# Linear attention before convolution in layer two of block 2: the order of three branches in a two-block fp32 kernel

## The chip, the cores and the metric

The kernel runs on one core of a Trainium2 chip. The metric is the device time of one execution in microseconds (us).

## The reference

Two blocks of two layers each work on 256 tokens of width 1024, batch 1, in fp32. Block 1 mixes three kinds of attention and is not touched. Block 2 takes block 1's output `x` and 256 context tokens. Each of its layers normalises both and projects them to a row of 15 chunks; three branches work on the chunks and are merged:

```
ya = conv_module(val, glu, gate)      # depthwise, 31 taps, layer norm, silu gate, @ w_conv_out
yb = gla_branch(...)                  # chunked linear attention, both directions, @ w_gla_out
yc = attn_branch(...)                 # 8 heads, keys of context and latent tokens, @ w_attn_out
merged = sigmoid(p13) * ya + sigmoid(p14) * yb + sigmoid(p15) * yc
xs = xs + gate_x * (merged @ w_out)   # layer one does the same for the context tokens
```

The sum has three terms and can be formed in any order. In layer two the context serves only as keys, values and state: the outputs are those of the 256 latent tokens.

## The kernel before

**Work and units.** Tokens lie in tiles of 128: tiles 0 and 1 are latent, 2 and 3 context. Layer one of block 2 works on four tiles throughout, layer two on four for the keys, values and decays and on two for the rest. Weights come in pieces of 256 rows by up to 512 columns (512 KB). A piece is loaded by SyncE's queue into one of four buffers (`w_raw`), split by ScalarE (`cut_hi`, L1749) and VectorE (`cut_lo`, L2131) into a high and a low part, for which there are three buffers, and multiplied on TensorE in three products, high by high, low by high, high by low (L1398 to L1400 in `project`, L1416 to L1418 in `project_t`). A chunk is four pieces. With two tiles, a `project` step is one tile and one piece, 6 matmuls of 512 columns; a `project_t` step is one block of 128 channels and one piece, 6 matmuls of 256 columns.

**The branches.** The convolution is numbered 0, linear attention 1 and attention 2. Branch 0 needs CGATE (its gate, by `project_t`), 1 needs GG, 2 needs AG. Each then has two chunks of merge gates, M0A and M0B, M1A and M1B, M2A and M2B, whose sigmoid goes to the `sigma` buffer (`ev_sig`, L1968), and an output product y0, y1 or y2 in two halves of two pieces each. `ev_y` multiplies a product with its sigma (L2485 for the branch that comes first, which writes `merged` directly, L2487 for the others) and `acc_add` on GpSimd (POOL) adds the others to `merged` (L2770).

**What runs beside them.** Linear attention is a chain across all engines: decays and their sums (L1576, L1584, L1593), transposes of queries and keys (L1313, `gla_kt` L2511), scores within a chunk (L1615), states (L1628, L2537), outputs (L1646, L1652), then a norm that ends in `gla_n` (L2559). The convolution is 124 taps on VectorE in layer two, 31 for each of four channel blocks (L2442, L2445), then a mean, a variance, a norm and the gate (`conv_g`, L2763), and a split into high and low (`conv_hi` L2005, `conv_lo` L2476). Attention has 8 maps for each of two query tiles: scores L1683, maximum, exponential (L2073), transpose (L1313), values (L1707).

**What sets the order.** `Plan` holds lists of steps. `second_main` is the main list: in layer two VAL, GLU, KKV, LRQ, GV and AQ, then the branches in the order of `BRANCHES`:

```
    for i in BRANCHES[l]:
        first, second = MERGE[i]
        if i == 0:
            yield from project_t(l, CGATE)
            yield from inp(first, tiles, sigma)
        elif i == 1:
            if l == LAYERS - 1:
                yield from inp(GG, tiles, gated)
            yield [("gated", l, GG, t) for t in tiles]
            yield from beside(inp(first, tiles, sigma), cut(i), 2)
        ...
        yield from y(i, 0)
        yield from inp(second, tiles, sigma)
        yield from y(i, 1)
```

`cut(i)` yields the transpose of each tile of the branch's gated result (`flip y1` or `flip y2`, L1313), and `beside(..., 2)` sets one behind every second step of the chunk. `gated` (POOL, L2776) multiplies the normalised result with the gate and comes ahead of the transpose. Linear attention, taps, convolution's end, head norms and attention are further lists. Each list is cut into lanes, one for each engine; a lane keeps its order. `Plan.order` plays the program through with estimated lengths (`LENGTH`) and always takes the step that can start first, ties by `rank`, in which taps come last and projections behind most others. The result is one fixed sequence for each engine, so on the chip a step that waits holds up all that stands behind it on its engine.

**Banks.** PSUM has eight banks: 0 to 3 for projections and output products (`proj2`), 4 to 6 for the rest, 7 for sums. The four blocks of CGATE hold all four projection banks from their first matmul until `ev_cg` (L1957) has read them. `ev_cg` writes to `b.cg`, which lies over the taps' source `conv_u`, and so waits for the last tap. `ev_gate` of GG (L1978) and `ev_sig` have no such wait. All branches of layer two share one buffer for their split operand, `b.y[1]`. `conv_hi` of layer two has no wait of its own for y1; it comes behind `conv_g`, which needs `ev_cg`.

**Pieces.** `Plan.weights` numbers the pieces in the order in which the lists use them and keeps for each the last step that reads it, which the load and the split of a later piece wait for. There are 304.

Of the kernel before, what the change touches and what calls it, by code (L numbers as in the profile page):

```python
# [84 lines left out]
MOD_COLS = 2 * 3 * KD  # L85
MERGE = [(M0A, M0B), (M1A, M1B), (M2A, M2B)]

BRANCHES = [(1, 0, 2), (0, 1, 2)]


def sigma_before(layer, c):

    order = [MERGE[i][half] for i in BRANCHES[layer] for half in range(2)]
    at = order.index(c)
# [3 lines left out]
def branch_before(layer, i):  # L98
    at = BRANCHES[layer].index(i)
    return None if at == 0 else BRANCHES[layer][at - 1]  # L100

# [195 lines left out]
def branch(kind):  # L297
    def steps(l, c, t):
        return [("ev_y", kind, l, c, t)] + ([] if int(kind[1]) == BRANCHES[l][0] else [("acc_add", kind, l, c, t)])
    return steps  # L300
# [19 lines left out]
def second_main(l):  # L320
# [13 lines left out]
    else:  # L334
# [5 lines left out]
        yield from inp(AQ, tiles, evacuate2)  # L340
    for i in BRANCHES[l]:
        first, second = MERGE[i]
# [147 lines left out]
class Plan:  # L490
# [10 lines left out]
    def weights(self):  # L501

        for _, steps in self.queues:
            for step in steps:
                if step[0] not in ("project", "project_t", "mod"):
                    continue
                name = step[1:5] if step[0] == "project" else ("in2", *step[1:4]) if step[0] == "project_t" else step[:4]
                if self.piece_of.get(name) is None or self.piece_of[name] != len(self.pieces) - 1:  # L510
                    self.piece_of[name] = len(self.pieces)
                    self.pieces.append(name)
                    self.last_step.append(step)
                self.last_step[-1] = step
        first_of_2 = next(n for n, name in enumerate(self.pieces) if name[0] == "in2")
        self.raw_slot, self.cut_slot, self.raw_before, self.cut_before = [], {}, [], {}
        self.raw_done, self.arrived = [], []
        in_raw, in_cut, loads, cuts, cutting = {}, {}, {}, 0, []
        for n, name in enumerate(self.pieces):
            if n == first_of_2:  # L520
                cuts = 0
            raws, slots = (RAW1, CUT1) if n < first_of_2 else (RAW2, CUT2)
            raw = (n if n < first_of_2 else n - first_of_2) % raws
            self.raw_slot.append(raw)
            self.raw_before.append(in_raw.get(raw))
            in_raw[raw] = n
            loads[raw] = loads.get(raw, 0) + 16
            self.arrived.append((f"weights_in{raw}", loads[raw]))
            if name[0] == "mod":
                self.raw_done.append(self.last_step[n])  # L530
                continue
            cut, cuts = cuts % slots, cuts + 1
            self.cut_slot[n], self.cut_before[n], in_cut[cut] = cut, in_cut.get(cut), n
            cutting += [("cut_hi", n), ("cut_lo", n)]
            self.raw_done.append(("cut_lo", n))
        self.queues += [(0, cutting), (0, [("load", n) for n in range(len(self.pieces))])]
# [1192 lines left out]
def scalar_engine(k):  # L1729
# [229 lines left out]
    def ev_sig(l, c, t):  # L1959
# [5 lines left out]
        else:  # L1965
            i, half = earlier
            act.wait_ge("ev_y" if i == BRANCHES[l][0] else "acc_add", f"y{i}", l, half, t)
        do(b.sigma[:, t, :], ps[:, :], ACT.Sigmoid).then_inc(sem["ev_sig"], 1)  # L1968
# [1084 lines left out]
```

## Time and profile before

| | us |
| --- | --- |
| median of 3 runs | 1483.71 |
| lowest and highest | 1481.89, 1485.86 |
| the profiled execution, its own time | 1480.43 |
| span of that execution | 1479.1 |
| TensorE busy | 1350.5 (91%) |
| VectorE busy | 865.4 (59%) |
| ScalarE busy | 632.1 (43%) |
| GpSimd busy | 283.4 (19%) |
| mean granted TensorE clock | 0.938 |

The rows further down are of the profiled execution; their times count from the start of its span. Engines are PE (TensorE matmul), PEld (its weight loads, which overlap PE), DVE (VectorE), ACT (ScalarE), POOL (GpSimd) and SP (SyncE, which issues the loads). A granted clock of 1.00 is 2.4 GHz, 0.50 is 1.2 GHz. A matmul's duration in the rows includes its way through the array, so neighbours overlap: the distance of two starts is what one costs in a dense row of them. "idle before <- releaser" is what ended the time in which an engine did nothing; "issue" is idle time for which the trace shows no wait.

### The profile page before, as it was taken

The page shows a single profiled execution, that of the slowest core. Times are in us where ns is not written, and L with a number is a line of the kernel's source. Part 1 is how long each engine was busy: PE and PEld are TensorE (multiplying, and loading weights), DVE is VectorE, ACT ScalarE, POOL GpSimd, SP SyncE. Part 2 cuts the span into 40 slices and gives each one's busy share as a digit, 9 for nine tenths or more (in the row PEclk, how much of TensorE's full clock was granted, in tenths as well). Part 3 has the DMA queues.
Part 4 walks back from the last instruction along what each step waited for, and adds up shares of the span by engine and source line. Part 5 has one row for each costly group of instructions (what it writes and reads, how often), then busy time and mean ns, then how long its engine had stood idle before and what let it go on. Part 6 is the DMA issues. An engine that isn't in the chain of part 4 may idle for free.

```text
span 1479.1 us, 18892 instructions
## 1 busy us (share of the span) xinstructions
PE 1350.5 (91%) x7490; PEld 1065.2 (72%) x7490; DVE 865.4 (59%) x1469; ACT 632.1 (43%) x1007; POOL 283.4 (19%) x224
## 2 busy tenths in 40 slices
PE   5999787999782999997999999999999979989997
PEld 4877675877671777776676887777898766667886
DVE  3885644885647233488996432234676796544554
ACT  3444623444625164322536442333562550556452
POOL 0200101200105221237000011311351251000112
PEclk9999897999895999999999999999999995799999
DMA  9542537432534221121111222223453220023552
GB/s 336 166 131 88 191 104 304 156 129 86 190 107 148 67 81 48 59 71 57 57 58 33 68 72 96 89 86 107 151 172 104 91 91 3 15 92 116 182 181 83
DMA packets 48040, 165.19 MB, mean 112 GB/s; under 512 B 5734, under 2 KB 6950, under 8 KB 47696
## 3 DMA queue, kind: packets, MB, share of 16 engines
q1 hardware_dynamic: 47952, 163.98, 33.9%
q8 instruction: 59, 0.97, 0.3%
q14 instruction: 29, 0.24, 0.1%
HBM read 162.91 MB, written 1.05 MB: 111 GB/s over the span
## 4 chain that ended last, share of the span: by engine, by line
PE 70%; issue 14%; DVE 7%; POOL 4%; DMA 3%; ACT 2%; SPq 0%; POOLq 0%; DVEq 0%; ACTq 0%
PE bank L1398 15%; PE bank L1399 14%; PE bank L1400 14%; PE bank L1313 3%; PE bank L1683 3%; PE bank L1707 2%; PE bank L1416 2%; PE bank L1417 2%; PE bank L1418 2%; DVE conv_val L2445 2%; DMA w_raw<-in_wm 2%; PE bank L1646 1%; PE bank L1652 1%; PE bank L1628 1%; DVE w_lo L2131 1%
## 5 line engine op out<-in xcount | busy, mean ns | idle before, releaser
L2131 DVE TENSOR_TENSOR w_lo<-w_raw,w_hi 128x1024 fp32r<-128x1024 f32 (+3 forms) x256 | 316.9, 1239 | 299.4 <-ACT w_hi L1749 299.0
L1398 PE MATMUL bank<-w_hi,x_hi 128*128 128x512 f32 (+4 forms) x1120 | 459.2, 410 | 14.5 <-DVE x_lo L2476 5.9
L1749 ACT ACTIVATE w_hi<-w_raw 128x1024 fp32r<-128x1024 f32 (+3 forms) x256 | 263.6, 1031 | 466.2 <-PE bank L1400 264.4
L1399 PE MATMUL bank<-w_lo,x_hi 128*128 128x512 f32 (+4 forms) x1120 | 430.7, 385 | 0.0
L1400 PE MATMUL bank<-w_hi,x_lo 128*128 128x512 f32 (+4 forms) x1120 | 430.6, 385 | 0.0
L1398 PEld LDWEIGHTS bank<-w_hi,x_hi 128*128 128x128 f32 x1120 | 214.7, 192 | 67.3 <-issue 16.3
L1400 PEld LDWEIGHTS bank<-w_hi,x_lo 128*128 128x128 f32 x1120 | 213.1, 190 | 42.9
L1399 PEld LDWEIGHTS bank<-w_lo,x_hi 128*128 128x128 f32 x1120 | 214.2, 191 | 36.1
L2445 DVE SCALAR_TENSOR_TENSOR conv_val<-conv_u,par,conv_val 128x512 f32<-128x512 f32 (+1 forms) x240 | 153.7, 691 | 0.0
L2770 POOL TENSOR_TENSOR merged<-merged,sigma 128x512 f32<-128x512 f32 x24 | 37.3, 1586 | 168.1 <-DVE sigma L2487 168.1
L1416 PE MATMUL bank<-x_hi,w_hi 128*128 128x512 f32 (+1 forms) x192 | 67.5, 352 | 0.4 <-ACT conv_val L1942 0.4
L1417 PE MATMUL bank<-x_hi,w_lo 128*128 128x512 f32 (+1 forms) x192 | 64.7, 337 | 0.0
L1418 PE MATMUL bank<-x_lo,w_hi 128*128 128x512 f32 (+1 forms) x192 | 64.7, 337 | 0.0
L2073 ACT ACTIVATE att_p<-bank,att_stat 128x512 f32<-128x512 f32 (+1 forms) x48 | 29.4, 615 | 60.4 <-DVE att_stat L2621 60.3
L1332 PE MATMUL bank<-w_raw,mod_c_padded 128*32 128x128 f32 x768 | 30.5, 303 | 26.8 <-DMA w_raw<-in_wm 26.7
L1707 PEld LDWEIGHTS bank<-gla_k_att_kv,att_pt 128*128 128x128 f32 x320 | 44.1, 202 | 9.5 <-issue 5.0
L1683 PE MATMUL bank<-att_k_t,att_q_t 64*128 64x512 f32 (+1 forms) x96 | 49.0, 616 | 0.5 <-DVE att_q_t L2611 0.5
L2763 POOL TENSOR_TENSOR conv_val<-conv_val,conv_u 128x512 f32<-128x512 f32 (+1 forms) x8 | 8.4, 1070 | 196.8 <-ACT conv_u L1957 155.7
L1332 PEld LDWEIGHTS bank<-w_raw,mod_c_padded 128*32 128x32 f32 x768 | 21.5, 119 | 33.1 <-issue 17.4
L1416 PEld LDWEIGHTS bank<-x_hi,w_hi 128*128 128x128 f32 x192 | 36.4, 190 | 9.4 <-issue 5.7
L1707 PE MATMUL bank<-gla_k_att_kv,att_pt 128*128 128x64 f32 x320 | 43.1, 280 | 0.0
L1394 PE MATMUL bank<-bias_parts,bias_sel 96*128 96x512 bf16 (+2 forms) x78 | 30.2, 387 | 12.8 <-DVE bias_parts L2387 12.8
(339 smaller groups left out, 1904.2 us busy)
## 6 DMA issues: line engine op xcount, KB each, us to landing
w_raw<-in_w SPq DMA_DIRECT2D x168, 512.0 KB, 3.5
w_raw<-in_wm SPq DMA_DIRECT2D x48, 512.0 KB, 3.8
w_raw<-in_wo SPq DMA_DIRECT2D x40, 512.0 KB, 3.6
w_raw<-in_wy_gla SPq DMA_DIRECT2D x8, 512.0 KB, 3.5
w_raw<-in_wy_conv SPq DMA_DIRECT2D x8, 512.0 KB, 3.5
w_raw<-in_wy_att SPq DMA_DIRECT2D x8, 512.0 KB, 3.5
w_raw<-in_w SPq DMA_DIRECT2D x8, 460.0 KB, 5.7
par<-in_small SPq DMA_DIRECT2D x2, 1218.0 KB, 6.7
```

The lines of the kernel that those rows point to most:

```text
L1332: ins = mm(k.bank[i][32 * j:32 * (j + 1), 0:P], m.c_pad[:, q, :], raw[:, kk, j * P:(j + 1) * P], start=q == 0, stop=q == KD - 1, tile_posi ...
L1398: mm(out, xh[:, q, col], hi[:, kk, 0:w], start=q == 0 and kind != "in2", stop=False)
L1399: mm(out, xh[:, q, col], lo[:, kk, 0:w], start=False, stop=False)
L1400: ins = mm(out, xl[:, q, col], hi[:, kk, 0:w], start=False, stop=last and kk == KP - 1)
L1416: mm(out, hi[:, kk, cols], b.xh[:, q, 0:n_tok], start=q == 0, stop=False)
L1417: mm(out, lo[:, kk, cols], b.xh[:, q, 0:n_tok], start=False, stop=False)
L1418: ins = mm(out, hi[:, kk, cols], b.xl[:, q, 0:n_tok], start=False, stop=q == KD - 1)
L1683: ins = mm(k.bank[i][:, g * keys:(g + 1) * keys], b.aq_t[rows, h % 4, qt * P:(qt + 1) * P], b.ak_t[rows, k0:k0 + keys], start=True, stop=True)
L1707: ins = mm(k.bank[i][:, at * HD:(at + 1) * HD], turned[:, (g * nb + c) * P:(g * nb + c + 1) * P], b.kkv[:, t, QK2 + P + kh * HD:QK2 + P + ...
L1749: do(hi, raw, ACT.Copy).then_inc(sem["cut_hi"], 1)
L2131: v.tensor_tensor(lo, raw, hi.bitcast(F32), ALU.subtract).then_inc(sem["cut_lo"], 1)
L2445: ins = v.scalar_tensor_tensor(out, src, taps[:, j, n:n + 1], out, ALU.mult, ALU.add)
```

## The change

The order of the branches in layer two becomes that of layer one: linear attention, convolution, attention. The main list of layer two behind AQ was CGATE, M0A, y0, M0B, y0, GG, M1A, y1, M1B, y1, AG, M2A, y2, M2B, y2. It is now GG, M1A, y1, M1B, y1, CGATE, M0A, y0, M0B, y0, AG, M2A, y2, M2B, y2. With it, y1 is the product that writes `merged` directly and y0 is added. `Plan.weights` now gives a piece a new number only when its name is new, where it did so whenever the name differed from the one before.

```
-BRANCHES = [(1, 0, 2), (0, 1, 2)]
+BRANCHES = [(1, 0, 2), (1, 0, 2)]
...
-                if self.piece_of.get(name) is None or self.piece_of[name] != len(self.pieces) - 1:
+                if name not in self.piece_of:
                     self.piece_of[name] = len(self.pieces)
                     self.pieces.append(name)
                     self.last_step.append(step)
-                self.last_step[-1] = step
+                self.last_step[self.piece_of[name]] = step
```

## Rows read from the trace of the kernel before

**Rows 1.** The page: busy time of the engines; TensorE and its granted clock in 40 slices.

```profile
PE 1350.5 (91%) x7490; PEld 1065.2 (72%) x7490; DVE 865.4 (59%) x1469; ACT 632.1 (43%) x1007; POOL 283.4 (19%) x224
...
PE   5999787999782999997999999999999979989997
...
PEclk9999897999895999999999999999999995799999
```

**Rows 2.** Stretches: us; PE, PEld, DVE, ACT, POOL busy (x); granted clock; DMA share; GB/s.

```profile
1187.90:1209.10 21.20, 19.57 (x139) 17.47 (x138) 19.87 (x32) 16.24 (x23) 14.68 (x9) 1.00 0.23 75
1209.10:1215.20 6.10, 0.00 (x0) 0.00 (x0) 6.10 (x7) 1.06 (x1) 4.91 (x4) 0.90 0.29 86
1215.20:1253.90 38.70, 35.30 (x212) 27.78 (x212) 24.39 (x59) 2.13 (x5) 3.96 (x4) 0.50 0.05 15
1253.90:1278.00 24.10, 23.86 (x59) 13.41 (x60) 14.40 (x32) 8.26 (x16) 3.06 (x3) 0.50 0.00 0
1278.00:1299.20 21.20, 21.20 (x109) 16.55 (x107) 11.91 (x21) 15.18 (x24) 1.44 (x2) 0.98 0.17 52
1299.20:1305.10 5.90, 0.01 (x1) 0.00 (x0) 2.03 (x4) 5.86 (x10) 1.41 (x2) 0.79 0.30 107
1305.10:1310.00 4.90, 4.88 (x15) 3.94 (x16) 0.80 (x3) 2.74 (x5) 0.00 (x0) 0.55 0.20 80
1310.00:1357.00 47.00, 47.00 (x235) 34.68 (x234) 22.58 (x34) 24.38 (x36) 0.00 (x0) 1.00 0.31 91
1357.00:1442.50 85.50, 85.50 (x385) 68.91 (x385) 44.29 (x41) 44.42 (x50) 17.40 (x10) 1.00 0.58 180
```

**Rows 3.** TensorE's waits from 1090 us to the end: us, times, longest.

```profile
PE bank L1615 <- issue: 6.2, 1, 6.2
PE bank L1398 <- DVE x_lo L2476: 5.9, 1, 5.9
```

**Rows 4.** TensorE in order of time: start, us, line, operation; 512-column projections, then CGATE's last.

```profile
1176.17 0.39 PE L1400 MATMUL bank<-w_hi,x_lo 128*128 128x512 f32 x1
1176.40 0.40 PE L1398 MATMUL bank<-w_hi,x_hi 128*128 128x512 f32 x1
...
1208.70 0.28 PE L1417 MATMUL bank<-x_hi,w_lo 128*128 128x256 f32 x1
1208.82 0.28 PE L1418 MATMUL bank<-x_lo,w_hi 128*128 128x256 f32 x1
1215.26 3.06 PE L1615 MATMUL bank<-gla_q_t,gla_k_t 64*128 64x128 f32 x16 [6.16 <-issue]
```

**Rows 5.** VectorE in order of time: taps, key transpose, first normalised tile, last tap, conv_lo.

```profile
1209.22 4.32 DVE L2445 SCALAR_TENSOR_TENSOR conv_val<-conv_u,par,conv_val 128x256 f32<-128x256 f32 x3
...
1214.48 0.68 DVE L2511 COPY gla_k_t<-bank 128x512 f32<-128x512 f32 x1
...
1252.35 0.68 DVE L2559 TENSOR_TENSOR gla_v<-gla_v,gla_ms 128x512 f32<-128x512 f32 x1
...
1271.35 0.48 DVE L2445 SCALAR_TENSOR_TENSOR conv_val<-conv_u,par,conv_val 128x256 f32<-128x256 f32 x1
...
1304.30 1.43 DVE L2476 TENSOR_TENSOR x_lo<-conv_val,x_hi 128x256 fp32r<-128x256 f32 x4 [0.99 <-ACT x_hi L2005]
```

**Rows 6.** ScalarE in order of time: the table load and the eviction of CGATE.

```profile
1273.91 1.28 ACT L1957 ACT_TABLE_LOAD   x1
1275.20 1.57 ACT L1957 ACTIVATE conv_u<-bank,par 128x256 f32<-128x256 f32 x4
```

**Rows 7.** Attention score groups, layer one (640 to 1040), layer two (1214 to 1278).

```profile
L1683 PE MATMUL bank<-att_k_t,att_q_t 64*128 64x512 f32 x32 | 17.4, 634 | 0.0
...
L1683 PE MATMUL bank<-att_k_t,att_q_t 64*128 64x512 f32 x12 | 12.1, 1124 | 0.5 <-DVE att_q_t L2611 0.5
```

**Rows 8.** Layer one: TensorE's longest wait, and the stretch behind it (columns of rows 2).

```profile
PE bank L1313 <- POOL gla_v L2776: 7.4, 1, 7.4
...
697.00:705.00 8.00, 6.15 (x22) 4.53 (x22) 7.96 (x8) 1.84 (x3) 8.00 (x6) 0.69 0.11 25
```

## The prediction

> **What bounds the kernel now.** I began with the page. TensorE is busy for 91% of the span, so only places where it waits or runs at the lower clock can give time. The slices of the last quarter show one such place: the granted clock falls to 0.5 and 0.7 of full in two neighbouring slices [rows 1]. That is layer two of block 2. I then cut it into stretches by what TensorE does [rows 2]. Up to 1209.1 us it projects the convolution gate (CGATE) beside the first steps of linear attention, at the full clock. Then it does nothing for 6.1 us. From 1215.2 to 1253.9 it works through linear attention alone, and to 1278.0 through attention alone, both at 0.50, the lower level (1.2 GHz against 2.4). From 1278.0 projections run again and the clock is back; 5.9 us more are lost at 1299.2, followed by 4.9 us at 0.55. From 1310 to 1442.5 TensorE is busy throughout at 1.00. There, order can give nothing.
>
> The list of TensorE's waits names both holes [rows 3]. The second is y0, the convolution's output product, which waits for the last step of the convolution (`conv_lo`, L2476). The first is listed as "issue", but the VectorE rows explain it: the linear attention product L1615 needs the key transpose `gla_kt`, which runs at 1214.48, behind three taps that took 4.32 us and a step of `gla_qi` [rows 4, 5].
>
> Why is there no projection to fill 1209 to 1278? The CGATE results hold all four projection banks until `ev_cg` has read them, and `ev_cg` waits for the last of the 124 taps, because it writes over the taps' source. The last tap runs at 1271.35, and ScalarE evicts CGATE at 1273.91 [rows 5, 6]. Only then can the next chunk (M0A) start. So the convolution, though first in the list, locks the main line for the 69 us from 1209 to 1278.
>
> **The change, part by part.** Weights, matmuls, evictions and DMAs stay the same in number; only layer two's order changes. SyncE's queue issues the same loads in another order and is idle enough: the DMA share is 0.58 in the dense stretch and 0.05 or less from 1215.2 to 1278.0 [rows 2]. The edit in `weights` does nothing here. Every piece has its steps in one unbroken run of the list, so the old test and the new one give the same numbering: 0 us.
>
> (1) GG (the linear attention's gate) takes CGATE's place: 48 matmuls of 512 columns at 0.23 us, 11.0 us, against 96 of 256 columns at 0.12 us, 11.5 us [rows 4]. I put 0. The start of linear attention therefore keeps its cover and its 6.1 us wait.
>
> (2) After GG comes M1A, but not all of it: the two transposes of the gated linear attention result (`flip y1`) stand after its second and fourth step in the same lane, and each needs linear attention to be finished. Before its end only two steps, 12 matmuls or 2.8 us, can go. If they fall in the 6.1 us wait they gain 2.8 us. If they fall in the half-clock stretch, where TensorE is 35.30 of 38.7 us busy, they cost about 5.2 us there and save 2.8 later, a loss of 2.4. I take 0 and keep both ends. What stays of the wait is at least 3.3 us.
>
> (3) GG's evictions are Silu on ScalarE and fall between linear attention's exponentials. One table load is 1.28 us [rows 6]; two of them would be 2.6 us. The load that CGATE needs in the middle of attention goes in exchange. VectorE, not ScalarE, is what is late there [rows 5], so I take 0 and keep 2.6 us as a loss.
>
> On the price of such a load, the row shows 1.28 us, with the eviction that needed it starting 0.01 us after its end, at 1275.20 [rows 6]. The Trainium skill ("ScalarE: Activation LUTs", "What ACT_TABLE_LOAD costs") adds a drain of about 1.38 us to each switch, 2.66 us in all. By it the loss in (3) would be bounded by 5.3 us and the sum below could be 5.3 us smaller. The trace shows no such gap behind the load, so the bound stays at 2.6.
>
> (4) From 1253.9 the rest of M1A, then y1, M1B, y1 and CGATE, are free to run between the attention products. The same products took 12.1 us for 12 in layer two and 17.4 us for 32 in layer one, 1.01 against 0.54 us each, a ratio of 0.54 [rows 7]. The 23.86 us of attention work shrink to 12.9 us: 11.2 us of the 24.1 are gained. The clock needs a while to return. The nearest row is 1305.1 to 1310.0, where it came back within 4.9 us of mixed projections and attention; those 4.9 us at the low level cost 2.3 us [rows 2]. Left: 8.9 us. If it stayed low for all of the stretch this term would be nearly 0.
>
> (5) The wait of 5.9 us for `conv_lo` goes, and the 4.9 us at 0.55 after it cost 2.7 instead (2.2 saved): 8.1 us. Between linear attention's end and y0 there will be 35 us or more of projections plus the attention, so the convolution's end chain, some 33 us from last tap to `conv_lo` (1271.35 to 1304.30) [rows 5], is covered. CGATE comes after the last tap and holds its banks for a moment only. If that cover were gone, the 5.9 us would be back.
>
> (6) A new wait: `flip y1` stands in TensorE's queue and waits for POOL's `gated`. Queued behind it are the rest of M1A and whatever attention steps the plan puts there. In layer one, which has this order already, that transpose waited 7.4 us and the clock then averaged 0.69 over 8 us [rows 8]. Layer two has two tiles instead of four and its first normalised tile is ready at 1252.35 [rows 5]; POOL has no query heads left by then. I take 1.5 us, bounds 0 and 10 (7.4 plus 31% of 8).
>
> Sum: 8.9 + 8.1 - 1.5 = 15.5 us. The profiled execution took 1480.4 us (span 1479.1, 1.3 around it), 3.3 us under the median of 1483.7. 1480.4 - 15.5 = 1464.9, and on the scale of the median **1468 us**.
>
> **The rivals.** A is the above: the 6.1 us wait stays, the clock drops, it returns with the projections. 1460 to 1475 us, chance 0.5.
>
> B: the two M1A steps fill enough of the wait, or the clock comes back with them, and linear attention runs at the full clock. For it: the clock was back 4.9 us after work resumed at 1305.1 [rows 2]. Against: the shortening leaves 3.3 us idle before a long row of small matmuls. TensorE's 35.30 us would be 19.1, but VectorE has 24.39 us of work in the same 38.7, so the stretch keeps at least 24.4: 14.3 more. With the 2.3 of (4) not paid: 32.1 us, about 1452; 1446 to 1458 us. Chance 0.27.
>
> C: the wait at `flip y1` is as large as in layer one. For it: the same code did this. Against: half the tiles, an emptier POOL. 8.5 us less than A: 1476.7, 1473 to 1482 us. Chance 0.17, a third of it within the measurement's reach of no change.
>
> D, slower: VectorE falls further behind in linear attention. The place is its queue between 1209 and 1254. Three taps took 4.32 us there [rows 5]; GG, M1A and y1 bring weight splits (`cut_lo`) there, and every microsecond of delay is now paid in full, since M1A stands behind `flip y1` and attention behind linear attention. It decides from 20 us of delay: 15.5 to eat the gain and 4.5 more. Against: the three slots for split weights are held full by M0A in this stretch today, so as many splits run in it, and VectorE is busy for 24.39 of 38.7 us only. Chance 0.06; at 22 us of delay it would be 1490 us.
>
> That the change does nothing is out: the list of branches decides layer two's order directly.
>
> **How the numbers follow.** A measurement of this kernel can tell about 0.3%, 4.5 us. Faster by more is below 1479.3: all of A and B, most of C, 0.88. The same: 0.07. Slower, above 1488.2: 0.05. The range takes in B and C but leaves B's best and D out: 1448 to 1479 us.
>
> **What would show it.** Right: the idle stretch before L1615 still 3 us or more; the clock at 0.5 in linear attention but 1.00 within about 5 us of the first M1A or y1 matmuls after it; L1398 matmuls between the attention products from linear attention's end; no wait for L2476; `ev_cg` within a few us of the CGATE matmuls. Wrong: the clock at 1.00 right through (B); TensorE waiting 5 us or more at L1313 for POOL L2776 in layer two (C); L1615 or L1646 waiting long for VectorE (D); CGATE's banks still held for the taps, which would void (5).

## The result, and the profile after

The changed kernel took **1462.59 us** (median of 4 runs, 1459.71 to 1471.77), the kernel before beside it 1483.04. The ratio is 0.988, 95% interval 0.9852 to 0.9907. The profiled execution took 1460.14 us, its span is 1458.8 and its mean granted clock 0.944, where before had 1480.43, 1479.1 and 0.938.

The page of the changed kernel: busy time of the engines, then TensorE's granted clock in 40 slices.

```profile
PE 1339.7 (92%) x7490; PEld 1057.8 (73%) x7490; DVE 865.4 (59%) x1469; ACT 630.2 (43%) x1006; POOL 283.6 (19%) x224
...
PEclk9999887999985899999999999999999997799998
```

As in [rows 1] the instruction counts of TensorE, VectorE and GpSimd are the same. TensorE is busy for 10.8 us less with the same 7490 matmuls: more of them ran at the full clock. The two low slices near the end are 7 and 7, where they were 5 and 7.

Stretches of the changed kernel, to be held against [rows 2] (us; PE, PEld, DVE, ACT, POOL busy with counts; granted clock; DMA share; GB/s):

```profile
1185.00:1210.60 25.60, 24.74 (x127) 17.87 (x125) 23.12 (x38) 22.26 (x29) 18.32 (x12) 1.00 0.25 81
1210.60:1214.10 3.50, 0.05 (x1) 0.00 (x0) 3.50 (x6) 1.06 (x1) 1.57 (x2) 1.00 0.34 135
1214.10:1251.00 36.90, 33.26 (x212) 26.18 (x212) 24.80 (x59) 2.03 (x5) 3.92 (x4) 0.55 0.08 29
1251.00:1258.60 7.60, 6.73 (x13) 3.37 (x13) 7.57 (x15) 2.76 (x5) 5.02 (x5) 0.50 0.01 2
1258.60:1270.00 11.40, 11.40 (x54) 8.20 (x53) 9.22 (x17) 5.74 (x9) 0.95 (x1) 0.98 0.15 47
1270.00:1305.00 35.00, 35.00 (x178) 26.77 (x176) 20.22 (x33) 25.64 (x38) 0.00 (x0) 1.00 0.31 105
1305.00:1337.00 32.00, 31.88 (x198) 24.66 (x198) 15.76 (x26) 16.00 (x28) 2.10 (x3) 1.00 0.30 100
1337.00:1422.00 85.00, 85.00 (x398) 68.78 (x397) 44.49 (x46) 44.61 (x55) 15.36 (x9) 1.00 0.53 167
```

Linear attention is the same work, 212 matmuls in both. The wait in front of it is 3.5 us instead of 6.2 (to the first L1615; the stretches are cut at 6.1), and the stretch at the low level ends at 1258.6 instead of at about 1278. From there TensorE is busy at 0.98 to 1.00 up to 1422; the hole of 5.9 us and the slow 4.9 us behind it are gone.

TensorE's waits from 1090 us to the end in the changed kernel (us in all, times, longest), against [rows 3]:

```profile
PE bank L1615 <- issue: 3.5, 1, 3.5
...
PE bank L1646 <- DVE gla_state L2537: 1.6, 1, 1.6
...
PE bank L1615 <- DVE gla_k_t L2511: 1.4, 1, 1.4
PE bank L1313 <- POOL gla_v L2776: 0.9, 1, 0.9
```

No wait for L2476 is left. `flip y1` (L1313 for POOL L2776) waits for 0.9 us. The rows of 1.6 and 1.4 lie inside linear attention and stood in the list of before too, with 1.6 and 0.9.

TensorE in order of time: the two M1A steps in front of the wait, and the way back of the clock behind linear attention (start, us, line, operation; idle time before it and its releaser in brackets).

```profile
1207.26 0.39 PE L1394 MATMUL bank<-bias_parts,bias_sel 96*128 96x512 bf16 x1
...
1210.26 0.39 PE L1400 MATMUL bank<-w_hi,x_lo 128*128 128x512 f32 x1
1214.14 2.57 PE L1615 MATMUL bank<-gla_q_t,gla_k_t 64*128 64x128 f32 x16 [3.49 <-issue]
...
1251.98 1.12 PE L1313 MATMUL bank<-ident,gla_v 128*128 128x128 f32 x4 [0.87 <-POOL gla_v L2776]
1253.02 3.78 PE L1683 MATMUL bank<-att_k_t,att_q_t 64*128 64x512 f32 x4
1256.73 0.79 PE L1398 MATMUL bank<-w_hi,x_hi 128*128 128x512 f32 x1
...
1258.61 0.63 PE L1399 MATMUL bank<-w_lo,x_hi 128*128 128x512 f32 x1
...
1259.31 0.40 PE L1398 MATMUL bank<-w_hi,x_hi 128*128 128x512 f32 x1
```

Twelve M1A matmuls end at 1210.6, and L1615 still starts at 1214.14. M1A goes on at 1256.73, behind the flip and four score products; its starts are 0.42 us apart until 1258.61 and 0.23 from 1259.31.

**The accounts.** The first product of the decays (L1566) starts at 1187.04 us before and at 1186.04 after. Up to there the two programs have the same steps in the same order, so this 1.0 us is not of the change's making. From there to the end it is 292.06 against 272.76 us: 19.3 us, where the prediction had 15.5. In these two stretches TensorE is busy for 266.69 and 255.75 us and idle for 25.37 and 17.01. So 10.9 us come from the same matmuls taking less time and 8.4 from less waiting. The waits named so far make 7.6 of the 8.4: the 5.9 before y0, 2.6 or 2.7 in front of L1615, and 0.9 the other way at the flip. Reckoning the clock by elapsed time comes out too high: 62.8 x 0.50 = 31.4 us before (1215.2 to 1278.0), 36.9 x 0.45 + 7.6 x 0.50 = 20.4 after, and 2.2 behind y0, 13.2 in all against the 10.9 found. Part of that is that the score products took 0.54 of their slow time at the full clock, not half of it [rows 7]; the rest is not explained.

The edit in `weights` has no run of its own. Worked out from the program text, the plan of the changed kernel has the same 304 pieces and the same steps in the same order with the old test and with the new one, so nothing above is due to it.

### The profile page after: what moved, and what is told of

Read it like the earlier page. It is cut to its first block, busy times and chain, and to the rows that moved or that the text cites. A ratio compares the mean times of both kernels' runs of the same rounds, so it can differ in the third digit from the quotient of the medians.

```text
span 1458.8 us, 18892 instructions
## 1 busy us (share of the span) xinstructions
PE 1339.7 (92%) x7490; PEld 1057.8 (73%) x7490; DVE 865.4 (59%) x1469; ACT 630.2 (43%) x1006; POOL 283.6 (19%) x224
## 4 chain that ended last, share of the span: by engine, by line
PE 69%; issue 14%; DVE 7%; POOL 4%; DMA 3%; ACT 2%; SPq 0%; POOLq 0%; DVEq 0%; ACTq 0%
PE bank L1398 15%; PE bank L1399 14%; PE bank L1400 14%; PE bank L1313 3%; PE bank L1683 3%; PE bank L1416 3%; PE bank L1707 2%; PE bank L1418 2%; PE bank L1417 2%; DVE conv_val L2445 2%; DVE w_lo L2131 1%; PE bank L1646 1%; PE bank L1652 1%; DMA w_raw<-in_wm 1%; PE bank L1628 1%
## 5 line engine op out<-in xcount | busy, mean ns | idle before, releaser
L1707 PEld LDWEIGHTS bank<-gla_k_att_kv,att_pt 128*128 128x128 f32 x320 | 41.3, 191 | 6.2 <-issue 3.5
L1683 PE MATMUL bank<-att_k_t,att_q_t 64*128 64x512 f32 (+1 forms) x96 | 45.1, 575 | 0.0
L1707 PE MATMUL bank<-gla_k_att_kv,att_pt 128*128 128x64 f32 x320 | 40.4, 269 | 0.0
```

The source lines that it names most:

```text
L1683: ins = mm(k.bank[i][:, g * keys:(g + 1) * keys], b.aq_t[rows, h % 4, qt * P:(qt + 1) * P], b.ak_t[rows, k0:k0 + keys], start=True, stop=True)
L1707: ins = mm(k.bank[i][:, at * HD:(at + 1) * HD], turned[:, (g * nb + c) * P:(g * nb + c + 1) * P], b.kkv[:, t, QK2 + P + kh * HD:QK2 + P + ...
```

## The experiments

My theory throughout was that the gain has two parts: main-line work that can run beside linear attention and attention and so brings the clock back, and the wait for `conv_lo`, which gets covered. All ratios are to the kernel before, run beside each kernel on the same chip. The line numbers of some kernels are 1 to 7 higher than those of the kernel before.

**1 and 2: without the bank lock, in the old and in the new order.** Layer two's CGATE result goes to two free tiles of `sigma` instead of onto the taps' source, so `ev_cg` need not wait for the last tap.

```
-    "ev_cg": lambda l, j: [("project_t", l, CGATE, NP - 1, j), ("tap", l, TAPS - 1, 3)],
+    "ev_cg": lambda l, j: [("project_t", l, CGATE, NP - 1, j),
+                           ("tap", l, TAPS - 1, 3) if l == 0 else ("acc_add", "y2", l - 1, 1, 3)],
...
+                b.sigma[:, 2:4, :].rearrange("p a b -> p (a b)").rearrange("p (c t) -> p c t", c=4)]
```

> Old order (convolution first), but in layer two CGATE is read into a place of its own, tiles 2 and 3 of the sigma buffer, and no longer waits for the last tap, so its four banks come free at once and M0A can run beside linear attention. My theory is that what the change brings is work from other branches that can run before the convolution is done; in the old order only M0A is free of it, then y0 stands and waits for the last step of the convolution. So: M0A moves into 1209 to 1254, attention's first half still has no projections beside it, and the wait before y0 grows by about what M0A takes, from 5.9 to 10 us or more. 1474 to 1480 us, a gain of 3 to 9. Rival: the held banks are all of it. Then this kernel gains 15 us or more, 1468 us or less.

> The changed kernel with the same edit: CGATE has a place of its own. In the changed kernel CGATE is projected long after the last tap (1270 against about 1300), so the lock should cost nothing there. My theory: within 2 us of the changed kernel, 1460 to 1466 us. Rival: ScalarE's or GpSimd's order still pays for the wait on the taps, then 1457 us or less.

Old order: 1477.16 us (1472.92 to 1480.83, 10 runs), ratio 0.9975 (0.9957 to 0.9993). New order: 1463.82 us (1462.08 to 1469.45), 0.9899 (0.9874 to 0.9924), the change's own time. Stretches of the first (columns as above):

```profile
1220.00:1230.00 10.00, 10.00 (x90) 7.59 (x88) 8.92 (x19) 2.96 (x4) 0.00 (x0) 1.00 0.33 105
1230.00:1240.00 10.00, 7.12 (x52) 5.23 (x49) 7.77 (x20) 2.70 (x4) 0.00 (x0) 0.73 0.36 107
...
1255.00:1278.00 23.00, 20.47 (x58) 11.06 (x56) 16.32 (x37) 6.85 (x15) 3.45 (x3) 0.57 0.00 1
```

Without the lock M0A runs inside linear attention and the clock is back at 1.00 there, but then the main list is at y0, which needs the end of the convolution, and attention is alone again at 0.57. No projection runs between 1231.6 and 1298.77, where y0 begins, 2.9 us after the first step of `conv_lo`. I had expected a wait of 10 us or more before y0. The trace shows none: what TensorE waited for in that stretch was attention itself (4.8 us in three waits for its exponentials). The lock is worth about 4 of 20 us in the old order and nothing that can be measured in the new one. What counts is how much of the main list does not depend on the convolution.

**3: both flips of y1 behind all of M1A.** M1A is then dense in linear attention instead of beside attention.

```
-            yield from beside(inp(first, tiles, sigma), cut(i), 2)
+            if l == LAYERS - 1:
+                yield from inp(first, tiles, sigma)
+                yield from cut(i)
+            else:
+                yield from beside(inp(first, tiles, sigma), cut(i), 2)
```

> The changed kernel with the two transposes of y1 behind the whole of M1A in layer two's list, where they stood behind its second and fourth step. All eight steps of M1A can then run before linear attention ends, 11 us of cover in place of 2.8. By my theory the stalls inside linear attention after the first L1615 (1.4, 1.6 us and small ones) fill, the clock comes back with the projections, and the 37 us from L1615 to linear attention's end shrink by 5 to 13 us: 1449 to 1458 us. The wait of 3.5 us before the first L1615 stays. Rival: the half clock there is set by that wait alone and the added projections run at half clock too: then linear attention ends 8 to 10 us later and the whole is within 3 us of the changed kernel, 1460 to 1466 us.

1464.51 us (1461.6 to 1469.08), 0.99 (0.9876 to 0.9925): no gain over the change. Its stretches and the wait that decided:

```profile
1220.00:1230.00 10.00, 10.00 (x92) 7.66 (x92) 7.59 (x17) 4.38 (x5) 0.00 (x0) 1.00 0.26 62
1230.00:1240.00 10.00, 6.91 (x54) 5.09 (x48) 7.45 (x20) 1.17 (x2) 0.00 (x0) 0.64 0.28 97
1240.00:1250.00 10.00, 9.47 (x56) 7.18 (x56) 4.33 (x9) 0.38 (x1) 3.58 (x3) 0.50 0.01 2
...
1260.00:1270.00 10.00, 10.00 (x29) 6.17 (x28) 7.99 (x17) 2.15 (x5) 2.68 (x3) 0.50 0.00 0
```

```profile
PE bank L1650 <- DVE gla_state L2541: 2.8, 1, 2.8
```

The clock came back in the first half and was lost again behind a wait of 2.8 us for a state, once M1A had run out. Projections were then missing beside attention until 1266.83, and the clock returned only at about 1270.

**4: the main list held back.** In the plan `flip y1` of layer two gets a dependence on an attention step, so the order stays but M1A comes late.

```
-        "y1": [("gated", l, GG, t)] + before_flip(l, 1),
+        "y1": [("gated", l, GG, t)] + before_flip(l, 1) + ([("a_v", l, 0, 4)] if l == LAYERS - 1 else []),
```

> The changed kernel, but the plan puts the first transpose of y1, and with it the rest of M1A and y1, behind the fifth map of attention's first tile. It puts back attention without projections beside it and nothing else. By my theory the clock stays at 0.50 through these maps as before the change, and 8 to 12 us of the gain go: 1470 to 1475 us. The y0 wait does not come back, because M1A, y1, M1B, y1 and CGATE still stand between. Rival: attention alone would get the full clock back by itself a few us after linear attention, then the loss is 4 us or less, 1467 us or less.

1478.73 us (1473.21 to 1480.82, 10 runs), 0.998 (0.9961 to 0.9999). It loses 16 us against the change by the medians (12 to 15 by the ratios), more than I expected. Two of its stretches, TensorE's longest wait, and ScalarE in order of time inside that wait:

```profile
1256.80:1277.00 20.20, 19.55 (x52) 11.35 (x53) 14.47 (x30) 4.75 (x11) 5.35 (x5) 0.50 0.00 1
...
1300.00:1311.00 11.00, 5.33 (x28) 4.29 (x26) 4.22 (x6) 10.64 (x14) 0.00 (x0) 0.90 0.26 74
```

```profile
PE bank L1313 <- ACT att_p L2073: 6.3, 2, 5.7
```

```profile
1297.52 1.28 ACT L1968 ACT_TABLE_LOAD   x1
1298.81 0.60 ACT L1968 ACTIVATE sigma<-bank 128x512 f32<-128x512 f32 x1
1299.43 1.28 ACT L1996 ACT_TABLE_LOAD   x1
1300.72 1.09 ACT L1996 ACTIVATE conv_val<-conv_val,par 128x256 f32<-128x256 f32 x2
...
1302.78 1.28 ACT L1968 ACT_TABLE_LOAD   x1
...
1304.69 1.28 ACT L1996 ACT_TABLE_LOAD   x1
```

Attention alone keeps the clock at 0.50 although TensorE is busy for 19.55 of 20.2 us. That is the price of term (4): without the main list beside it, attention has the low level in this order too. The second loss is one I had not thought of. M1A's sigmoids, pushed later, meet the convolution's activations. ScalarE changes its table four times from 1297.52 to 1304.69, attention's exponentials stand behind that, and TensorE waits 5.7 us for them. From 1311 to 1340 it then has a mean clock of 0.92, 2.3 us more. An estimate from these figures: 16.1 less 5.7 less 2.3 leaves about 8 us for attention without projections. The wait before y0 did not come back, as expected.

The kernel before has such a pile in front of its y0 as well, which I had overlooked: table loads for M0A's sigmoids and the convolution's activations in turn, at 1296.81, 1298.72 and 1302.07, and ScalarE busy for 5.86 of the 5.90 us in which TensorE waits [rows 2]. How much of that wait they made, no run separates.

**5: the last six taps ahead of the key transpose go behind it.** It aims at the wait before L1615.

```
-    "tap": lambda l, n, j: [("tap", l, n - 1, j), ("conv_u", l, j)],
+    "tap": lambda l, n, j: [("tap", l, n - 1, j), ("conv_u", l, j)] + (
+        [("gla_kt", l, 0)] if l == LAYERS - 1 and 4 * n + j >= 73 else []),
```

> The changed kernel, with the six taps that the plan put ahead of gla_kt in VectorE's queue put behind it (a tap from number 73 on waits for gla_kt in the plan). Nothing else is asked for. My theory: the wait of 3.5 us before the first L1615 is VectorE's lateness and it alone takes the clock down, since TensorE's work behind it keeps the clock where it is. Then the wait is 1 us or less, linear attention runs at 1.00 up to its end, and the stretch from L1615 on shrinks by 10 us or more: 1447 to 1455 us. Rival: the clock goes down there anyway, because linear attention without projections cannot hold it (the short waits of 1.4 and 1.6 us behind it are enough). Then only the wait goes, 2 to 4 us: 1458 to 1462 us.

1461.79 us (1459.05 to 1465.32), 0.9872 (0.985 to 0.9893). The wait is 2.4 us instead of 3.5, where I had expected 1 or less, and two small ones came up behind it (1.0 and 0.7 us before L1629, a state product). The clock was lost all the same: 0.50 in 1210 to 1215, 0.83 and 0.68 up to 1230, 0.50 from there. The taps are one cause of the wait, not the only one, and removing a third of it does not save the clock.

**6: taps planned at 1.2 us instead of 0.66.** Only the estimate in the plan changes; the kernel places them elsewhere.

```
+        if step[0] == "tap" and step[1] == LAYERS - 1:
+            return 1.2
         return LENGTH.get(step[0], 0.1)
```

> The changed kernel, with a tap of layer two planned at 1.2 us in place of 0.66 (alone on VectorE one takes 0.4, beside GpSimd's work up to 1.4). The plan then puts fewer taps ahead of linear attention's steps: 47 in place of 83 at its scores. My theory: the waits for VectorE in linear attention nearly go (3.5, 1.4, 1.6 and 0.5 us now), with the same effect on the clock as in the run before, 1446 to 1455 us. The taps end later, about 1300, which M1B and y1 cover. Rival: the taps end so late that CGATE's banks are held for them again; a wait of 5 us or more comes back before M0A or y0 and the whole is 1462 us or more.

1484.56 us (1479.47 to 1489.71, 10 runs), 1.0031 (1.001 to 1.0051): the whole gain is gone. TensorE's waits:

```profile
PE bank L1400 <- DVE x_lo L2478: 7.1, 1, 7.1
PE bank L1396 <- ACT conv_u L1959: 6.5, 1, 6.5
```

VectorE in order of time, the last taps:

```profile
1346.49 1.65 DVE L2447 SCALAR_TENSOR_TENSOR conv_val<-conv_u,par,conv_val 128x256 f32<-128x256 f32 x4
```

The plan lets the taps trail, and the last four start at 1346.49 and end at 1348.1, as VectorE's rows in order of time have it; the table load of `ev_cg` starts right behind them, at 1348.19. CGATE has caught up with the taps, as in the old order: its banks are locked until then and M0A waits 6.5 us, then y0 waits 7.1 us for the end of the convolution. The lock and the wait before y0 are both back in the new order. Linear attention got little for it: the waits before its score products are still 3.0 us (4.9 in the change), the one before L1648 is still 1.6, and the clock is 0.50 from 1220 to 1260. So term (5) rests on the taps being done when CGATE comes. In the change the last ones start at 1268.99 and `ev_cg` runs at 1332.96, a margin of 64 us.

**7 and 8: a better version.** AG, attention's gate, comes right behind GG; with it both flips go behind M1A (experiment 3). The eighth adds the edit of experiment 5.

```
                 yield from inp(GG, tiles, gated)
+                yield from inp(AG, tiles, gated)
...
-            yield from inp(AG, tiles, gated)
+            if l < LAYERS - 1:
+                yield from inp(AG, tiles, gated)
```

> The changed kernel with AG (attention's gate) projected right behind GG and the transposes of y1 behind the whole of M1A: 22 us of projections that need nothing from linear attention. In the run with the transposes behind M1A alone the clock came back at 1219 with the projections and fell again at 1231, when they ran out and TensorE waited 2.85 us. Here some stand between linear attention's two output products too. My theory: the clock stays at 1.00 in more of that stretch; 4 to 8 us less than the changed kernel, 1454 to 1459 us. Rival: as in that run, what is run early is missing later, beside attention, and the low clock only moves: 1460 to 1466 us.

> Both edits together: the taps behind gla_kt, AG early, the transposes behind M1A. If the low clock comes from the waits and the lack of projections together, this one holds 1.00 through linear attention and attention's start, and is the fastest: 1442 to 1450 us. If the two gains are the same gain, it is within 3 us of the better one of the two.

The seventh took 1456.32 us (0.983, 0.9811 to 0.985, without one of its four runs, which took 2617.88 us and is not explained). The eighth took **1453.31 us** (1452.19 to 1453.99), 0.9812 (0.9798 to 0.9827), and is faster than the kernel before and than the change. Against the seventh the intervals overlap, so the third edit isn't shown to add anything. I had expected 1442 to 1450. Stretches of the seventh:

```profile
1216.60:1230.00 13.40, 13.40 (x77) 11.06 (x78) 10.54 (x20) 1.66 (x2) 0.00 (x0) 0.75 0.34 98
1230.00:1260.00 30.00, 30.00 (x230) 22.64 (x229) 24.08 (x51) 11.01 (x15) 6.79 (x5) 1.00 0.32 97
1260.00:1270.00 10.00, 6.39 (x21) 3.91 (x19) 9.94 (x20) 4.04 (x8) 3.94 (x3) 0.76 0.16 54
```

TensorE is busy for all of 1230 to 1260, at 1.00. Linear attention runs at the full clock to its end, with projections between its products, which no kernel so far had. The work that is late is then VectorE's, 9.94 of 10 us busy behind it. The trace of the eighth says why it missed its forecast. The wait before the first score product is gone (0.2 us), but the same taps, four in 4.49 us, now stand behind `gla_kt`, and the next transpose waits for a VectorE step that stands behind them (us in all, times, longest):

```profile
PE bank L1320 <- DVE gla_att L2527: 3.9, 1, 3.9
PE bank L1320 <- DVE x_lo L2148: 3.5, 1, 3.5
```

Behind each of the two waits TensorE works at 0.50, from 1217 to about 1221 and from 1264 to about 1279. The lateness moved, and with it the low clock.

**9 to 11: which edit does it, and how sure are the differences.** AG early alone, the change itself, and the eighth kernel again, in one session.

> The changed kernel with one edit: AG, attention's gate (8 steps, 48 matmuls of 512 columns, 11 us at the full clock), is projected right behind GG in layer two instead of behind y0, and the two flips of y1 stay where the change has them. It separates the two edits that together made 1456.3: the flips alone made 1464.5 against the change's 1462.6. Theory: the gain belongs to the pair. With AG alone the work in front of linear attention grows by 11 us, but only two steps of M1A can go before linear attention's end, so its small matmuls run without cover at 0.50 again; what AG gains is the wait before the first scores product that it fills (3.5 us, at most) and the clock level at which its 11 us run there, against the same 11 us at the full clock taken from the dense end. Expected 1459 to 1463, clock near 0.50 from about 1230 to 1258. Rival: it is AG that does it, and the flips do nothing: 1454 to 1458, with the clock at 1.00 in linear attention. If the wait before the first scores product is still 3 us or more, AG has filled nothing there, and the time should be that of the change, 1462 to 1464.

> The changed kernel as it is, on the same chip and beside the same runs of the kernel before as the kernel with AG early and the one with three edits. Its times so far reached from 1459.7 to 1471.8, a width of 0.8%, so differences of 2 to 4 us between it and its variants rest on it. Theory: its median stays between 1460 and 1465 and the ratio to before at 0.986 to 0.990; the same three waits before L1615, at the key transpose and at L1646 are seen in the profile. Rival: another session gives it 1466 or more; then the variants that I read as equal to it (gate without the lock 1463.8, flips behind M1A 1464.5) would be gains of their own.

> The fastest kernel so far again (six taps behind the key transpose, flips of y1 behind M1A, AG early; it took 1453.3), now beside the change itself in one session. Theory: it is a gain of its own of 8 to 10 us over the change, ratio to before 0.979 to 0.983, and the profile shows the clock above 0.50 for most of linear attention (1221 to 1258) and low only for a short stretch behind it (1262 to 1280). Rival: the gain was one of the session, and the two kernels are within 3 us of each other.

Over 6 runs each: AG alone 1464.08 us (1449.5 to 1465.51), 0.9869 (0.9833 to 0.9904); the change 1466.28 (1460.84 to 1468.05), 0.9898 (0.9871 to 0.9926); three edits 1456.14 (1449.63 to 1459.54), 0.9826 (0.9798 to 0.9853). The three edits are 10.1 us better than the change, and in their trace the clock is 0.83 in 1220 to 1230, 1.00 from 1230 to 1270 and 0.83 in 1270 to 1280. AG alone can't be told from it: 2.2 us with overlapping intervals. The change measured 1.3 us more than I had allowed, but its ratio is that of experiments 2 and 3 (0.9899, 0.99), so they can't be told from it. Its new trace has the three waits again (3.5, 0.9 and 1.6 us), but the clock is 0.50 from 1220 to 1260, where the first trace had short spells of 1.00 up to 1225, and the span is 5.4 us longer. AG alone, in stretches:

```profile
1230.00:1240.00 10.00, 10.00 (x90) 7.57 (x89) 9.01 (x19) 3.20 (x4) 0.00 (x0) 1.00 0.34 107
1240.00:1250.00 10.00, 7.64 (x64) 5.49 (x60) 7.55 (x20) 1.06 (x1) 0.00 (x0) 0.83 0.32 106
```

I expected 0.50 from about 1230. In the trace the clock held to about 1246 and was 0.50 from 1250; it fell behind a wait of 2.4 us for a state, the same place as in experiments 1 and 3. Its wait before the first score product was still 3.5 us. Eleven microseconds of AG, or of M1A, or of M0A cover half of linear attention each; the pair covers all of it. That fits 3 and 9 giving little alone and some 8 us together.

## Why the prediction was right, and where its sizes were off

It said 1468 us with case A; measured were 1462.59, in A's band of 1460 to 1475. The median of the later session was 1466.28. The mechanism of A is what the traces show, with two readings to correct, in (4).

**(1) GG for CGATE, 0.** Held: from the first L1566 to the first L1615 it is 28.2 us before and 28.1 after, though M1A's two steps are now in it. **(2) The two M1A steps, 0 with bounds +2.8 and -2.4.** This term was mis-sized. The steps ran at 1207.26 to 1210.6 and the wait fell from 6.2 to 3.5 us: 2.7, next to the upper bound of 2.8. "What stays of the wait is at least 3.3" was right. The wait is filled ahead, since its end is set by VectorE: `gla_kt` (L2511) at 1213.37, behind four taps in 4.07 us.

**(3) Table loads, 0.** Held: GG's evictions brought two loads, at 1201.02 and 1208.58, but both lie in the 28.1 us of (1), ahead of linear attention's products, and cost nothing there. In the whole kernel ScalarE has 1006 instructions for 1007. In the changed kernel CGATE's load and its first activation read

```profile
1331.67 1.28 ACT L1957 ACT_TABLE_LOAD   x1
1332.96 1.20 ACT L1957 ACTIVATE conv_u<-bank,par 128x256 f32<-128x256 f32 x3
```

The activation starts 0.01 us behind the load's end. The drain of 1.38 us that the Trainium skill adds ("ScalarE: Activation LUTs", "What ACT_TABLE_LOAD costs") doesn't show here either. Nor does it show ahead of a load: in the rows of experiment 4 the activation from 1298.81 ends at 1299.41 and the next load starts at 1299.43. That loads can hurt is shown by experiment 4, by their number in one place.

**(4) Attention at the full clock, 8.9, and (5) y0, 8.1.** From the 19.3 us go 2.7 for (2) and 1.4 for linear attention itself, which took 33.9 us from L1615 to its end instead of 35.3, since the clock fell later (0.55 on average, not 0.50); 0.9 was paid at the flip. That leaves 16.1 for (4) and (5), where I had 17.0. It is a remainder, not a measurement of each. What (5) counted went as a whole, which would leave 8.0 for (4); experiment 4 gives about 8 as well. The clock was back at 1258.6, which I had put at 1258.8, and that is luck: linear attention ended 2.5 us earlier, M1A began only at 1256.73, behind the flip and four score products, and then it took 2 us, not 4.9. The other reading to correct is who brought the clock back in the kernel before. I wrote that projections run again from 1278.0. They don't; TensorE in order of time there:

```profile
1275.19 3.75 PE L1542 MATMUL bank<-conv_val,mean_w 128*128 128x256 f32 x8
1278.76 1.01 PE L1707 MATMUL bank<-gla_k_att_kv,att_pt 128*128 128x64 f32 x8
...
1280.09 0.58 PE L1398 MATMUL bank<-w_hi,x_hi 128*128 128x512 f32 x1
```

Eight value products (L1707) took 1.97 us up to then and take 1.01 at 1278.76. The clock was back ahead of the first projection, behind eight matmuls of the convolution's mean (L1542), which come once the last tap is done.

The cover of (5) is shown both ways: no wait in the change, and 6.5 and 7.1 us where the taps trail (experiment 6). Experiment 1 shows that the bank lock, on which the first part of the prediction leans, was the smaller part of the matter: freed alone, it gave 4 us, since y0 stood behind it.

**(6) The new wait, 1.5.** It was 0.9.

**Rivals.** C is out by that 0.9. (The stated range, 1448 to 1479, also left out C's upper end, 1482, which its text does not say.) D's mechanism (VectorE late) is real in experiment 6, by another place: not linear attention but the taps. B did not happen in the change. Against it I had given the idle time left and the row of small matmuls; which of the two took the clock, no run separates. But B is a real state of this kernel: with enough work put inside linear attention the clock is 1.00 from 1230 to its end (experiments 7, 8 and 11). That the time is then 1453.31, next to B's 1452, is in part chance, since the low clock came up again behind it.

## What to carry to other kernels

Where small matmuls on a dependence chain run alone, ask which large matmuls are ready at that moment and put the branch first whose following work depends on least. Freeing a lock is worth little if the next piece of the list waits for the same late result. Work given to one gap is taken from another: count how much a stretch needs before moving it, as one filler covered half of linear attention and two covered all.

## What the runs showed that I had not expected

**Being busy is not enough for the clock.** TensorE was busy for 19.55 of 20.2 us in attention alone and was granted 0.50 throughout (experiment 4). In the change it came back within 2 us of the first projection matmuls, in experiment 3 within 4, but in experiment 8 only 12 us after the first (1267.01), with twelve of them in two groups between attention's products. Projections are not the only work that does it. In the kernel before and in experiment 4 the clock rose while the convolution's mean ran, in the latter at 1278.0, and there it stayed at 1.00 for the 5 us of attention and transposes alone behind it (1279.0 to 1284.0). Waits of 2.4 to 2.9 us for `gla_state` stood before three falls from 1.00 to 0.50 (experiments 1, 3, 9); whether the wait or the small matmuls behind it did it was not separated.

**The spread between runs goes with the clock.** AG alone took 1449.5 us once, with a mean clock of 0.956, and 1460.75 to 1465.51 in the other five, with 0.942 to 0.946. Span times clock is 1448.2 x 0.956 = 1384 in that run and 1462.8 x 0.942 = 1378 in the next, so all of its lead lies in the clock. What made it keep the clock in that run isn't known, as only one other run has a trace. Differences of 2 or 3 us between variants mean nothing in four runs.

**Taps are slower beside some of GpSimd's work.** The same tap at two places of the changed kernel, VectorE in order of time, and the engines' busy time in four stretches in which VectorE runs taps:

```profile
1208.77 4.07 DVE L2445 SCALAR_TENSOR_TENSOR conv_val<-conv_u,par,conv_val 128x256 f32<-128x256 f32 x4
...
1268.99 1.66 DVE L2445 SCALAR_TENSOR_TENSOR conv_val<-conv_u,par,conv_val 128x256 f32<-128x256 f32 x4
```

```profile
1208.77:1212.80 4.03, 1.88 (x9) 1.15 (x7) 4.03 (x6) 2.75 (x3) 3.40 (x3) 1.00 0.60 214
1268.99:1270.65 1.66, 1.66 (x9) 1.34 (x9) 1.66 (x5) 1.65 (x2) 0.00 (x0) 1.00 0.30 94
```

```profile
1220.42:1221.29 0.87, 0.87 (x14) 0.87 (x12) 0.87 (x4) 0.00 (x0) 0.00 (x0) 1.00 0.90 363
1258.33:1259.83 1.50, 1.50 (x7) 1.17 (x6) 1.50 (x2) 0.00 (x0) 1.22 (x1) 0.74 0.00 0
```

Four taps took 4.07 us where POOL is busy for 3.40 of 4.03 us, and 1.66 where it is idle. DMA traffic is higher in the first stretch too, but it is not the cause. Two taps at 1220.42 take 0.87 us with POOL idle beside 363 GB/s, and a single one at 1258.33 takes 1.50 beside POOL's `gated` (L2776) with no traffic at all. In the traces before and after, all 164 taps from 1100 us on with POOL idle took 0.46 to 0.48 us each. Beside POOL's products of 512 columns a tap took up to 1.5 us; beside its steps of 4 columns (L2817) it took 0.48. It is the stretch at 1208.77 that delays the key transpose and holds up linear attention.
